# Block products by seven in the down projection of two feed-forwards

## What is computed

```python
def swiglu(h, wg, wu, wd):
    return (jax.nn.silu(h @ wg) * (h @ wu)) @ wd
# four of them: x = x + swiglu(rms_norm(x), ...), twice with a factor 0.5; the hidden width is 2816

def memory_cross_attention(h, mem_n, wq, wk, wv, wo, g_q, g_k):
    ...
    k = rms_norm((mem_n @ wk).reshape(B, M, MEM_HEADS, HEAD_DIM), g_k)
    v = (mem_n @ wv).reshape(B, M, MEM_HEADS, HEAD_DIM)
```

## Time and profile before

| | us |
|---|---|
| median of 3 runs (1193.67 to 1194.36) | 1193.91 |
| the profiled execution | 1194.76 |
| its span in the profile | 1192.9 |
| TensorE busy | 1185.8 |
| TensorE weight loads busy | 985.0 |
| VectorE busy | 693.2 |
| ScalarE busy | 562.5 |
| GpSimd busy | 68.0 |

### The profile page before, as it was taken

The page is one execution under the profiler, slowest core; times in us unless marked ns, Lnnn a source line. Parts: engine busy times, 40 slices in busy tenths (PEclk is TensorE's granted clock), DMA queues, the critical chain, the costliest instruction groups (busy, mean ns, idle before and its releaser), DMA issues.

```text
span 1192.9 us, 14801 instructions
## 1 busy us (share of the span) xinstructions
PE 1185.8 (99%) x6098; PEld 985.0 (83%) x6098; DVE 693.2 (58%) x752; ACT 562.5 (47%) x718; POOL 68.0 (6%) x129
## 2 busy tenths in 40 slices
PE   8999999999999999999999999999999999999998
PEld 6888888888889988888888888888888776888887
DVE  6677465545366766656546545545675876545452
ACT  7644354434246554544434443534536734534431
POOL 2100000000010002000001000000210020000000
PEclk9999999999999999999999999999999999999999
DMA  8754457565566235674655556464645543465560
GB/s 282 282 181 159 153 182 232 168 212 209 179 220 239 107 106 196 215 244 156 226 183 171 188 187 202 157 239 129 208 154 177 142 159 106 141 212 165 189 212 36
DMA packets 147908, 217.95 MB, mean 183 GB/s; under 512 B 5209, under 2 KB 115841, under 8 KB 147713
## 3 DMA queue, kind: packets, MB, share of 16 engines
q1 hardware_dynamic: 144864, 206.69, 52.0%
q0 software_dynamic: 2976, 10.31, 2.6%
HBM read 215.93 MB, written 1.05 MB: 182 GB/s over the span
## 4 chain that ended last, share of the span: by engine, by line
PE 97%; DVE 1%; ACT 1%; DMA 1%; SPq 0%; issue 0%; POOL 0%; DVEq 0%; POOLq 0%
PE acc L1968 29%; PE acc L1970 29%; PE acc L1969 29%; PE turn L1961 5%; DMA X<-in_x 1%; PE acc L2587 1%; PE acc L2631 1%; PE turn L2098 1%; PE turn L2441 1%; PE turn L2184 1%; PE acc L2206 1%; PE acc L2464 1%; PE turn L2343 0%; PE turn L2444 0%; DVE w_lo L1248 0%; ACT w_hi L834 0%
## 5 line engine op out<-in xcount | busy, mean ns | idle before, releaser
L1252 DVE TENSOR_TENSOR w_lo<-raw,w_hi 128x2048 fp32r<-128x2048 f32 (+1 forms) x170 | 383.4, 2278 | 159.0 <-ACT w_hi L837 158.8
L1968 PE MATMUL acc<-w_hi,xt 128*128 128x512 f32 (+2 forms) x1088 | 426.8, 392 | 1.1 <-DVE w_lo L1368 0.9
L1970 PE MATMUL acc<-w_hi,xt 128*128 128x512 f32 (+2 forms) x1088 | 419.4, 385 | 0.0
L1969 PE MATMUL acc<-w_lo,xt 128*128 128x512 f32 (+2 forms) x1088 | 418.7, 385 | 0.0
L837 ACT ACTIVATE w_hi<-raw 128x2048 fp32r<-128x2048 f32 x174 | 326.6, 1906 | 129.1 <-PE acc L1970 113.1
L1968 PEld LDWEIGHTS acc<-w_hi,xt 128*128 128x128 f32 x1088 | 204.5, 188 | 42.6 <-issue 2.1
L1970 PEld LDWEIGHTS acc<-w_hi,xt 128*128 128x128 f32 x1088 | 204.3, 188 | 41.5
L1969 PEld LDWEIGHTS acc<-w_lo,xt 128*128 128x128 f32 x1088 | 204.7, 188 | 38.8 <-issue 0.2
L882 ACT ACTIVATE sg<-acc,rstd 128x256 f32<-128x256 f32 x88 | 36.9, 471 | 239.3 <-PE acc L1970 239.3
L1334 DVE SCALAR_TENSOR_TENSOR hh<-acc,rstd,sg 128x256 f32<-128x256 f32 x88 | 38.5, 480 | 174.7 <-ACT sg L882 174.7
L1968 PE MATMUL acc<-w_hi,ht 128*128 128x512 f32 x352 | 138.0, 392 | 0.0
(11 more groups left out here) (291 smaller groups left out, 916.4 us busy)
## 6 DMA issues: line engine op xcount, KB each, us to landing
raw<-in_ffn_w_gate_up SPq DMA_DIRECT2D x88, 512.0 KB, 4.8
raw<-in_ffn_w_down SPq DMA_DIRECT2D x22, 1024.0 KB, 5.0
raw<-in_ffn_wg SPq DMA_DIRECT2D x44, 512.0 KB, 3.9
raw<-in_ffn_wu SPq DMA_DIRECT2D x44, 512.0 KB, 4.9
raw<-in_ffn_wd SPq DMA_DIRECT2D x22, 1024.0 KB, 5.0
raw<-in_a_w_in SPq DMA_DIRECT2D x14, 1024.0 KB, 5.7
raw<-in_w_in SPq DMA_DIRECT2D x10, 1024.0 KB, 5.8
raw<-in_a_w_out SPq DMA_DIRECT2D x8, 1024.0 KB, 5.0
```

What stands on the lines that cost most here:

```text
L1252: V.tensor_tensor(w_lo[:, u % RING, 0:kt * w], raw[:, raw_at["unit", u], 0:kt * w], w_hi[:, u % RING, 0:kt * w].bitcast(F32), ALU.subtract ...
L1968: mm(o, lhs[0], rhs[0], start=start, stop=False)
L1969: mm(o, lhs[0], rhs[1], start=False, stop=False)
L1970: return mm(o, lhs[1], rhs[0], start=False, stop=stop)
```

## The change

In feed-forwards 0 and 3 the down units 1, 3, 5 and 6 are computed with seven block products (the scheme of Strassen and Winograd). With A the 256x256 piece of the hidden rows and B the unit as 2x2 blocks, seven products of sums take the place of eight: three go on adding in `acc` banks, four add up over the four units in the four `turn` banks. This adds:

- GpSimd, for each of the four hidden blocks: four sums of 128x128 (`s1` to `s4`), from a copy that ScalarE makes of the transposed bank into `xn`; ScalarE and VectorE split them into `xt[1]`.
- GpSimd, for each seven unit: four sums of 128x512 (`t1` to `t4`) from `raw` into `xn`, linked by a semaphore each; they wait for `s_lo` of the seven unit before.
- Such a unit has seven quarters in place of four and takes two slots of the ring; ScalarE and VectorE split it in three steps (three quarters, the first sum, three sums). `fitting` and `up_to` keep the units brought up within the ring.
- After unit 6: ScalarE copies one bank, VectorE adds the four banks into X (`seven_to_rows`) before the residual.

Two smaller changes. Hidden blocks are transposed in pairs, after every second block, in all four feed-forwards; `sg` is dropped and `hh` has four buffers. Memory keys and values are loaded as two units of 4 row tiles with 256 columns of each, so that their matmuls have 512 columns.

```diff
-    U_MKV = narrow(ins["mem_wk_2"])
-    narrow(ins["mem_wv_2"])
+    U_MKV = len(units)
+    for k0 in (0, 4):
+        units.append((4, BLK, [(0, part(ins["mem_wk_2"], k0 * P, 4, 0, 256)), (256, part(ins["mem_wv_2"], k0 * P, 4, 0, 256))]))
...
+    SEVEN = {0: (1, 3, 5, 6), 3: (1, 3, 5, 6)}
+    SEVEN_F = sorted(SEVEN)
+    SEVEN_U = [U_FFN[f][1] + i for f in SEVEN_F for i in SEVEN[f]]
+    at_slot, slot_of = [], []
+    for u in range(N_UNITS):
+        at_slot.append(len(slot_of))
+        slot_of += [(u, part_) for part_ in range(2 if u in SEVEN_U else 1)]
...
+    def fitting(n, used):
+
+        ends = at_slot + [len(slot_of)]
+        while ends[n] - RING > at_slot[used]:
+            n -= 1
+        return n
...
+            def seven_sums(f):
+
+                base = 4 * SEVEN_F.index(f)
+                tt = nc.gpsimd.tensor_tensor
+                a12, a22, a11, a21, s1, s3, s2, s4 = [x_flat[:, k * P:(k + 1) * P] for k in range(8)]
+                for j in range(4):
+                    pool.wait_ge(s_xf, base + j + 1)
+                    if j:
+                        pool.wait_ge(s_slo, base + j)
+                    link(tt(s1, a21, a22, ALU.add))
+                    link(tt(s2, s1, a11, ALU.subtract))
+                    link(tt(s3, a21, a11, ALU.subtract))
+                    tt(s4, a12, s2, ALU.subtract).then_inc(s_ssum, 1)
+                    pool.wait_ge(s_ssum, base + j + 1)
+                for j in range(4):
+                    u = SEVEN_U[base + j]
+                    at = raw_at["unit", u]
+                    if j:
+                        pool.wait_ge(s_lo, SEVEN_U[base + j - 1] + 1)
+                    else:
+                        pool.wait_ge(s_slo, base + 4)
+                    pool.wait_ge(s_loaded[at], arrived["unit", u])
+                    b21, b22, b11, b12 = [raw[:, at, k * BLK:(k + 1) * BLK] for k in range(4)]
+                    t2, t3, t1, t4 = [x_flat[:, k * BLK:(k + 1) * BLK] for k in range(4)]
+                    link(tt(t1, b12, b11, ALU.subtract))
+                    link(tt(t2, b22, t1, ALU.subtract))
+                    link(tt(t3, b12, b22, ALU.subtract))
+                    tt(t4, b21, t2, ALU.subtract).then_inc(s_tsum, 1)
+                    pool.wait_ge(s_tsum, base + j + 1)
+
+            seven_sums(0)
...
+                    slot_free(u, 0)
+                    if u in SEVEN_U:
+                        n7 = SEVEN_U.index(u)
+                        nc.scalar.activation(w_hi[:, slot(u), 0:3 * BLK], raw[:, at, 0:3 * BLK], ACT.Copy).then_inc(s_swhi, 1)
+                        act.wait_ge(s_tsum, n7 + 1)
+                        nc.scalar.activation(w_hi[:, slot(u), 3 * BLK:], x_flat[:, 0:BLK], ACT.Copy).then_inc(s_swhi, 1)
+                        slot_free(u, 1)
+                        nc.scalar.activation(w_hi[:, slot(u, 1), 0:3 * BLK], x_flat[:, BLK:], ACT.Copy).then_inc(s_hi, 1)
+                        continue
...
+                    if b >= 4:
+                        act.wait_ge(s_turned, tr[b - 4][0] + 1)
...
-                    if b >= 1:
-                        high(tr[b - 1][0], pair(ht_hl, 0, 2 * (b - 1)))
+                    split_to(up_to(f, b))
+                    if b >= 2 and b % 2 == 0:
+                        for done_b in (b - 2, b - 1):
+                            if done_b in SEVEN.get(f, ()):
+                                act.wait_ge(s_turned, tr[done_b][0] + 1)
+                                nc.scalar.activation(x_flat[:, 0:BLK], tb[tr[done_b][0] % 4][:], ACT.Copy).then_inc(s_xf, 1)
+                            high(tr[done_b][0], pair(ht_hl, 0, 2 * done_b))
+                    if f in SEVEN and b >= 3 and b % 2 == 1:
+                        j = (b - 3) // 2
+                        act.wait_ge(s_ssum, 4 * SEVEN_F.index(f) + j + 1)
+                        nc.scalar.activation(seven_rows(0, j), x_flat[:, BLK:2 * BLK], ACT.Copy).then_inc(s_shi, 1)
+                    if f in SEVEN and b >= FFN_NB - 2:
+                        split_to(U_FFN[f][1] + SEVEN[f][0] + b - FFN_NB + 3)
...
+                if f in SEVEN:
+                    n = F[f]["sums"]
+                    act.wait_ge(s_turned, n + 1)
+                    nc.scalar.activation(x_flat[:, 0:BLK], tb[n % 4][:], ACT.Copy).then_inc(s_afree, 1)
...
+                    if u in SEVEN_U:
+                        n7, at = SEVEN_U.index(u), raw_at["unit", u]
+                        dve.wait_ge(s_swhi, 2 * n7 + 1)
+                        V.tensor_tensor(w_lo[:, slot(u), 0:3 * BLK], raw[:, at, 0:3 * BLK],
+                                        w_hi[:, slot(u), 0:3 * BLK].bitcast(F32), ALU.subtract)
+                        dve.wait_ge(s_swhi, 2 * n7 + 2)
+                        V.tensor_tensor(w_lo[:, slot(u), 3 * BLK:], x_flat[:, 0:BLK],
+                                        w_hi[:, slot(u), 3 * BLK:].bitcast(F32), ALU.subtract)
+                        dve.wait_ge(s_hi, u + 1)
+                        V.tensor_tensor(w_lo[:, slot(u, 1), 0:3 * BLK], x_flat[:, BLK:],
+                                        w_hi[:, slot(u, 1), 0:3 * BLK].bitcast(F32), ALU.subtract).then_inc(s_lo, 1)
+                        continue
...
+            def seven_to_rows(n, factor):
+
+                p1, u2, u3 = [x_flat[:, k * BLK:(k + 1) * BLK] for k in range(3)]
+                dve.wait_ge(*freed(n))
+                dve.wait_ge(s_turned, n + 4)
+                V.tensor_tensor(u2, tb[(n + 1) % 4][:], p1, ALU.add).then_inc(s_tfree, 1)
+                dve.wait_ge(*freed(n + 1))
+                V.tensor_tensor(u3, tb[(n + 2) % 4][:], u2, ALU.add).then_inc(s_tfree, 1)
+                link(V.scalar_tensor_tensor(X[:, 0, :], x_flat[:, 0:2 * BLK], factor, X[:, 0, :], ALU.mult, ALU.add))
+                dve.wait_ge(*freed(n + 2))
+                for half in range(2):
+                    rows = X[:, 1, half * BLK:(half + 1) * BLK]
+                    link(V.scalar_tensor_tensor(rows, u3, factor, rows, ALU.mult, ALU.add))
+                for t in range(TT):
+                    rows = X[:, t, BLK:]
+                    last = V.scalar_tensor_tensor(rows, tb[(n + 3) % 4][:], factor, rows, ALU.mult, ALU.add)
+                    if t == 0:
+                        link(last)
+                last.then_inc(s_tfree, 1)
+                dve.wait_ge(*freed(n + 3))
...
+            def seven_unit(f, j, u, i, c):
+
+                base, n = 4 * SEVEN_F.index(f), F[f]["sums"]
+                pe.wait_ge(s_slo, base + j + 1)
+                at = [2 * ((c + half) % 2) + t for t, half in ((0, 0), (0, 1), (1, 0))]
+                rows = {(t, k): [ht[:, hl, 2 * i + k, t * P:(t + 1) * P] for hl in range(2)] for t in range(TT) for k in range(2)}
+                s1, s3, s2, s4 = [[seven_rows(hl, j, m, 1) for hl in range(2)] for m in range(4)]
+                quarters = [[w[:, slot(u, q // 4), q % 4 * BLK:(q % 4 + 1) * BLK] for w in (w_hi, w_lo)] for q in range(7)]
+                steps = ((2, None, rows[0, 1]), (3, None, s2), (0, at[0], rows[0, 0]), (1, at[1], s4),
+                         (4, None, s3), (5, None, s1), (6, at[2], rows[1, 0]))
+                for m, (q, bank, lhs) in enumerate(steps):
+                    if bank is None:
+                        k = (2, 3, 4, 5).index(q)
+                        o = take(n + k) if j == 0 else tb[(n + k) % 4]
+                        last = product(o[:], lhs, quarters[q], j == 0, j == 3)
+                        if j == 3:
+                            last.then_inc(s_turned, 1)
+                    else:
+                        last = product(acc[bank][:], lhs, quarters[q], False, False)
+                    if m == 3:
+                        last.then_inc(s_sused, 1)
+                return last
...
+                    if i in SEVEN.get(f, ()):
+                        seven_unit(f, SEVEN[f].index(i), u0 + i, i, c).then_inc(s_used, 1)
+                    else:
+                        unit(i, [0, 1]).then_inc(s_used, 1)
...
-                turn_hidden(0)
                 for b in range(2, FFN_NB):
                     by_columns_block(u0 + 2 * b, c0 + b, xt_hl(0))
-                    turn_hidden(b - 1)
+                    if b % 2 == 0:
+                        turn_hidden(b - 2)
+                        turn_hidden(b - 1)
...
+            def memory_product(i, t, ks=range(4)):

                 pe.wait_ge(s_lo, U_MKV + i + 1)
                 for k in ks:
-                    last = product(acc[2 - 2 * t][:, i * 256:(i + 1) * 256],
-                                   [xt[1][:, hl, k, t * P:(t + 1) * P] for hl in range(2)],
-                                   weights(U_MKV + i, k, 256), k == 0, k == KD - 1)
-                if t == 1 and ks[-1] == KD - 1:
+                    last = product(acc[2 - 2 * t][:], [xt[1][:, hl, 4 * i + k, t * P:(t + 1) * P] for hl in range(2)],
+                                   weights(U_MKV + i, k, BLK), (i, k) == (0, 0), (i, k) == (1, 3))
+                if t == 1 and ks[-1] == 3:
```

(28 more changed lines are left out.)

73 lines of the change are left out of this document (43 added, 30 removed).

## The result

The changed kernel takes 1210.21 us (median of 4 runs, 1209.39 to 1212.07) against 1194.07 (median of 4) for the kernel before, run beside it. The ratio is 1.0136, with a 95% interval of 1.0124 to 1.0149: slower by 16.1 us, where the forecast was 11.3 slower (1205.2) and the range reached to 1216. The profiled execution took 1210.45, its span is 1208.7.

The account below looks back on a forecast made before the run. TensorE, busy 1185.8 of 1192.9 us, was taken as the bound. From the profiled 1194.76, savings of 5.44, 0.5 and 0.8 and added waits of 2 x 9.0 gave 1206.0, or 1205.2 as median; range 1190 to 1216.

Parts of the forecast that it names:

- The saving: TensorE: seven products 5.44 us, merged memory keys and values 0.5, paired transposes 0.8; together 6.7 us less.
- The chain: Down stage: GpSimd sums, ScalarE roundings and VectorE subtractions in turn deliver unit 6 at T+40.9; waits total 9.0 us per feed-forward.
- T: The end of the last gate/up block of a feed-forward, from which the forecast counts its times in us.
- The first wait: TensorE halfway through down unit 0 waits for VectorE's gated product: 2.9 us in each of two feed-forwards.
- The price of a sum: A 128x512 two-input sum on GpSimd, not in the trace, taken as two copies: 1.23 us, bounds 0.61 and 1.47.
- The upper price: A GpSimd sum as three passes, two reads and a write: 1.47 us, for which the forecast gave 1215.6 us.
- The second wait: TensorE waits before down unit 6 for VectorE's last subtraction: 6.0 us in each of two feed-forwards.
- The term that was left at nothing: TensorE's clock falling to 1.2 GHz after the wait before unit 6: a rival at 0.26, middle 1210, up to 1214.7.
- the prediction's own signs of being wrong: No idle time in the down stages, GpSimd sums near 0.6 us, or a lower granted clock in those slices.
- (A): Rival: the other engines keep up and the kernel is faster, 1188 with sums at 0.61, 1190 without exclusion; chance 0.17.
- (B): Rival: close to no change, with a GpSimd sum near 0.93 us, 1192 to 1196 us; chance 0.08.
- (D): Rival: sums dearer still, or transfers bind once raw slots are held longer, 1213 to 1220 us; chance 0.08.

Follow-up runs that it names:

- short sums: Changed kernel with GpSimd's weight sums made over only 128 of 512 columns, the other columns left out; 1187.82 us.
- The filler before the first wait: Changed kernel with 10 extra matmuls on TensorE ahead of the wait halfway through down unit 0 only; 1210.5 us.
- the kernel with filler: Changed kernel with extra matmuls on TensorE in feed-forwards 0 and 3: 10 ahead of the wait halfway through down unit 0, 24 ahead of unit 6; 1205.75 us.
- The memsets: Changed kernel with each GpSimd weight sum of a seven unit replaced by a memset about as long that reads nothing; 1192.55 us.
- the kernels at 1188: Changed kernel with weight sums on VectorE (1187.91 us), with sums over 128 columns (1187.82), or with three seven units in place of four (1188.68).

## Why the prediction was right, and where it was short

*The saving.* 24 matmuls at 0.2266 and the small changes, 6.7 together: from 1194.25 to 1187.91 with the sums on VectorE is 6.3, from 1194.3 to 1187.82 with short sums 6.5. Right to 0.4.

*The chain.* The schedule had GpSimd's first sum free to run at T-3.4, s_lo of unit 1 at T+5.6, the gated product at T+6.5, s_lo of unit 3 at T+17.2, of unit 5 at T+30.1 and of unit 6 at T+40.9. The trace, with T = 276.90, has T-3.6 (271.92 + 2.69 - 1.29), T+5.65 (280.79 + 1.76), T+6.4 (282.46 + 0.87), T+17.6 (292.77 + 1.76), T+30.3 (305.45 + 1.76) and T+41.0 (316.18 + 1.76). The first wait was to be 2.9 and is 2.9 (283.39 - 280.51, the end of the matmul before by its rate).

*The price of a sum.* 1.23 was taken, two copies; it is 1.29. The estimate from the Trainium skill (GPSIMD Engine Reference, section 3.1) was 1.26, nearer. By 16 sums that should have put s_lo of unit 6 1.0 later, and it came at T+41.0, not T+41.9. The trace has the reason: an operation that was held by the other engine needs less after its release than it lasts alone. Five sums end 1.14 to 1.16 after VectorE's subtraction and not 1.29, 0.7 in all; three subtractions end 2.14, 2.15 and 1.62 after the sum that held them, where 2.25, 2.25 and 1.75 were counted, 0.35 in all. What else differs, the 0.5 at unit 3 among it, comes to 0.2. So two errors of about 1 us cancelled, and that T+40.9 came out so exactly is in part luck. The upper price was also summed wrongly: 0.24 more on 16 sums is 3.8 in each feed-forward, so 1.47 gives 1212.9 and not 1215.6.

*The second wait.* 6.0 was forecast, 4.55 measured (318.04 - 313.49). Unit 6 came on time; TensorE came 1.7 later, since after the first wait the clock fell to 1.2 GHz for nine matmuls, seven whole steps of 0.43 and parts of two more; from 283.39 to the transposes at 287.84 it lost 1.7 against 12 steps of 0.2266. The filler before the first wait gives them back, and the second wait grows, 5.58 for 4.39 of idle time, with the total unchanged. So this loss of clock is covered: 2.9 + 1.7 + 4.55 is 9.15, and 9.0 of waits were forecast.

*The term that was left at nothing.* What the sum lacked is the clock after the second wait, which had been given a chance of 0.26 as a rival and a middle of 1210. The measured 1210.2 lies in the band of the forecast (1199 to 1211) as well as at that middle, so the time alone doesn't tell them apart; the granted clock does, and a lower one was among the prediction's own signs of being wrong. From the start of unit 6, 70 steps from matmul to matmul are 15.86 us at full rate (70 x 0.2266). In feed-forward 0 they took 17.56 (318.04 to 335.60), in feed-forward 3 18.85 (1175.90 to 1194.75): 1.7 and 3.0 more, together 4.7.

```profile
335.60 0.39 PE L2109 MATMUL acc<-w_lo,ht 128*128 128x512 f32 x1
...
1175.90 0.76 PE L2108 MATMUL turn<-w_hi,ht 128*128 128x512 f32 x1 [4.39 <-issue]
...
1194.75 0.39 PE L2109 MATMUL acc<-w_lo,ht 128*128 128x512 f32 x1
```

That is nearly the distance between 1205.2 and 1210.2, and the kernel with filler, at 1205.75, measures it as 4.5. The two agree only roughly: in the kernel with filler unit 6 also comes 0.4 earlier in each feed-forward. Why the slow stretch is longer in feed-forward 3 no run shows. The likeliest case was therefore the wrong one of two neighbours: with a wait of 6 us in the forecast the clock should have gone into the sum and not beside it, although no row of the trace before showed such a wait.

*The other rivals.* (A) needed a sum below 0.93 or no exclusion. Both conditions were made on the chip. A sum of 0.94 gives 1192.59, inside the 1192 to 1196 of (B); the small changes alone give 1192.85, so this is also the break-even against a kernel without seven units. Without exclusion it is 1192.55, where 1190 had been forecast. Of these 2.5 the waits make 1.6: from start to start they are 1.4 and 0.7, and 1.2 and 0.1 were forecast. The memsets last 1.30 where the forecast had 1.23, and at unit 5 ScalarE waits for slots of the ring (3.5 before its first rounding, 0.65 before its last), which the schedule didn't count. Another 0.7 is the time without waits, 1187.9 where 1187.2 was counted. (D), transfers that bind, didn't show: with more work on the same raw slots TensorE's list of waits of the kernels at 1188 has none for a transfer into the raw slots.

## What to carry to other kernels

When one engine is busy to 99%, a trade of its work for work elsewhere is decided by the slowest chain of the others, laid out against the times at which the full engine asks for its parts; totals (GpSimd 13% busy, VectorE 60%) say nothing about it. Put elementwise work with two SBUF inputs on VectorE if it has the room, even if GpSimd idles: here 32 sums moved onto the engine that looked busier turned 16 us lost into 6 us gained. And count a wait of several microseconds on TensorE with the slow matmuls that follow it.

## What the runs showed of the hardware

- GpSimd's two-input operation: 0.46 us for 128 columns, 0.94 for 352, 1.29 for 512, which is 2.16 ns a column and 0.18 us fixed; VectorE does 512 in 0.69.
- A GpSimd operation that only writes (memset of 1434 columns, 1.30) neither delays nor is delayed by VectorE's two-input subtractions (2.28 beside it); one that reads is held until the subtraction ends, up to 3.22 for 1.29, and holds a later subtraction in turn, 3.02 for 2.29. A held sum ends 1.14 to 1.16 after its release, where it lasts 1.29 alone. The Trainium skill (SBUF — State Buffer, section SBUF: two separate sides) confines the lock of VectorE's two-input operations to GpSimd operations that read SBUF; the memsets agree.
- The clock fell to 1.2 GHz (0.50) with waits of 4.4 us, after which TensorE took 1.7 and 3.0 us longer, and also with waits of only 2.7 us, in both feed-forwards (1.7 and 1.5 us longer). In the two kernels with a wait of 1.3 us, the memsets and the sums over 352 columns, it stayed at 1.00.
